# Forget heads' values computed as feature tiles inside the attention, and a new place for the bias strips' source

## The chip, the cores and the metric

The kernel runs on 1 core of one Trainium2 chip. The metric is the device time in microseconds (us) of one execution. Three executions of the kernel before took 2245.96, 2246.1 and 2246.89 us (median 2246.1).

## The reference, cut to what matters

Two blocks run one after the other on 512 tokens of width 1024. The first has two layers (L0 and L1) of attention and feed-forward, and the change touches only these and the scratch memory of the second block (M).

```python
proj = h @ w_in[l]                                   # h: 512 x 1024, normed
qa, ka, va, qb, kb, vb, f_logit = jnp.split(proj, split_at, axis=-1)   # six parts of 512, one of 8
oa = diff_attention(rotary(qa), rotary(ka), va, lam) # 4 heads, two maps each, values 128 wide
oa = rms_norm(oa, diff_sub_g[l]) * (1.0 - lam_init)
ob = forgetting_attention(qb, kb, vb, log_sigmoid(f_logit + forget_bias[l]))  # 8 heads of 64
x = x + rms_norm(concat(oa, ob) @ w_out[l], attn_post_g[l])
x = x + rms_norm((silu(h2 @ w_gate[l]) * (h2 @ w_up[l])) @ w_down[l], ffn_post_g[l])
```

The forgetting attention adds a decay to the scores, the difference of cumulated log forget gates. The second block has an attention with a relative position bias. It reads this bias from strips in device memory (8 heads x 128 rows x 512 words), which the kernel writes near its start.

## The kernel before, in words

All engines run hand-ordered programs, and waits on counters tie them together. SyncE (SP) streams 512 KB weight slabs in the order of a list, `plan`, into four raw buffers. A slab's transfer may be issued once the slab four places before it has been split. ScalarE (ACT) copies each slab to a rounded high part (L1532), and VectorE (DVE) subtracts to get the low part (L927). There are three buffers for such pairs. TensorE (PE) then makes three matmuls for each product (high by low, low by high, high by high).

Two shapes of product are used. A **token tile** (`token_tiles`, L633 to L635) holds 128 tokens by 512 columns of the output. It takes slabs of 2 x 128 rows by 512 columns, so that a row of a slab is 2 KB long. Four token tiles need 96 matmuls. A **feature tile** (`feature_tile`, L593) holds 128 columns by 512 tokens. It takes a slab of 8 x 128 rows by 128 columns, so that a row is 512 B long, and needs 24 matmuls.

In each layer PE makes the forget tile, the first tile of `qa` and of `ka` with their rotations (L735), then `va` as four token tiles, the small transposes of the log forget gates (L746), `vb` as four token tiles, and the sums of the log gates (L752). DVE copies the even token tiles into `V` (L1188), and ACT the odd ones (L1694). Both do so after they have split all slabs up to three places past the last `va` slab, or `vb` slab (`slabs_of`, `splits_for`). DVE then writes the negated sums (L1194), from which GpSimd (POOL) makes the decay rows. Slabs are counted from 0 here: forget, `qa`, `ka`, four of `va` (3 to 6), and then in the kernel before four of `vb` (7 to 10).

The attention (`attend`) runs 32 steps, steps 0 to 15 for the four differential heads and steps 16 to 31 for four pairs of forget heads, four query tiles each. In step i, PE makes the scores of step i (L661, L666), then what `fill(i)` gives it, the transposes of the weights of step i - 3 (L677), and, for every second step, the products with the values of step i - 4 (L690). Six more turns end it. `FILL` puts the remaining 14 feature tiles of `qa`, `ka`, `qb` and `kb` into the turns 0, 1, 4, 5, 8, 9, 13, 15, 17, 19, 21, 23, 25 and 27. Within a turn DVE reduces the scores to their maximum (L990 in a forget step), ACT takes the exponentials (L1583), DVE the reciprocals of the sums (L1004), POOL scales the weights (L1943), and PE transposes them. DVE and ACT copy the transposed weights to memory (L1020, L1600), and the results of the forget heads go to `MIXED` by ACT (L1609) and DVE (L1041). PSUM has eight banks: seven go round in the order of use during the attention, and the last holds the products with the values.

At its start POOL issues nine small loads for the second block (`BVR`, `BFG`, `W2C`; L1951 to L1954), and then one transfer of 2 MB that writes the bias strips (L1958). Its source is `REVB`, 8 partitions of 640 words in the arena, where rows of the attention's weights lie later. DVE and ACT therefore wait for that transfer before L0's attention.

## Time and profile before

| | |
|---|---|
| median of three executions | 2246.1 us |
| the profiled execution, its own time | 2241.13 us |
| its span, from first to last instruction | 2239.8 us |
| TensorE busy | 2119.8 us (95%) |
| VectorE, ScalarE, GpSimd busy | 988.2, 814.8, 227.0 us |
| mean granted TensorE clock | 0.987 |

The page gives the busy time of each engine and the groups of instructions; the trace behind it gives each instruction with its start and the wait before it. With TensorE busy nearly all the time, the waits on TensorE are what is to be read, and the time counts that lie between two of its landmarks. Starts are in us from the span's start.

### The profile page before, as it was taken

The page shows a single profiled execution, that of the slowest core. Times are in us where ns is not written, and L with a number is a line of the kernel's source. Part 1 is how long each engine was busy: PE and PEld are TensorE (multiplying, and loading weights), DVE is VectorE, ACT ScalarE, POOL GpSimd, SP SyncE. Part 2 cuts the span into 40 slices and gives each one's busy share as a digit, 9 for nine tenths or more (in the row PEclk, how much of TensorE's full clock was granted, in tenths as well). Part 3 has the DMA queues.
Part 4 walks back from the last instruction along what each step waited for, and adds up shares of the span by engine and source line. Part 5 has one row for each costly group of instructions (what it writes and reads, how often), then busy time and mean ns, then how long its engine had stood idle before and what let it go on. Part 6 is the DMA issues. An engine that isn't in the chain of part 4 may idle for free. (4 is left out here: it accounts for less than half of the span.)

```text
span 2239.8 us, 25576 instructions
## 1 busy us (share of the span) xinstructions
PE 2119.8 (95%) x10364; PEld 1703.8 (76%) x10364; DVE 988.2 (44%) x1833; ACT 814.8 (36%) x1574; POOL 227.0 (10%) x256
## 2 busy tenths in 40 slices
PE   6899899999998999999999998999798999999997
PEld 5667688888887767688888887878655788888886
DVE  6265453323336375453323336645456444323333
ACT  4145442222234255452222225344256334222322
POOL 3003410000000004310000000000156101000000
PEclk9999999999999999999999999999999999999999
DMA  6521123333322311223233332322411233333321
GB/s 155 110 76 57 57 73 109 97 97 97 103 86 69 108 43 63 67 84 102 92 99 97 96 98 58 98 57 81 104 43 38 67 111 92 94 97 101 94 92 68
DMA packets 273721, 192.10 MB, mean 86 GB/s; under 512 B 22060, under 2 KB 241364, under 8 KB 273604
## 3 DMA queue, kind: packets, MB, share of 16 engines
q1 hardware_dynamic: 268704, 177.76, 27.2%
q0 software_dynamic: 4752, 12.67, 2.4%
q8 instruction: 82, 1.34, 0.2%
q14 instruction: 35, 0.29, 0.0%
q10 hardware_dynamic: 148, 0.04, 0.0%
HBM read 186.21 MB, written 4.23 MB: 85 GB/s over the span
## 5 line engine op out<-in xcount | busy, mean ns | idle before, releaser
L593 PE MATMUL bank<-h_features,weights_hi_lo 128*128 128x512 f32 (+1 forms) x5160 | 1131.4, 380 | 9.5 <-POOL h_features L1915 7.8
L593 PEld LDWEIGHTS bank<-h_features,weights_hi_lo 128*128 128x128 f32 x5160 | 928.7, 189 | 196.0 <-issue 14.8
L927 DVE TENSOR_TENSOR weights_hi_lo<-weights,weights_hi_lo 128x1024 fp32r<-128x1024 f32 (+1 forms) x337 | 402.5, 1198 | 702.2 <-ACT weights_hi_lo L1532 701.7
L1532 ACT ACTIVATE weights_hi_lo<-weights 128x1024 fp32r<-128x1024 f32 (+1 forms) x337 | 341.0, 1016 | 393.1 <-PE bank L635 346.2
L633 PE MATMUL bank<-weights_hi_lo,hidden 128*128 128x512 f32 x528 | 205.4, 389 | 0.0
L634 PE MATMUL bank<-weights_hi_lo,hidden 128*128 128x512 f32 x528 | 205.4, 389 | 0.0
L635 PE MATMUL bank<-weights_hi_lo,hidden 128*128 128x512 f32 x528 | 205.4, 389 | 0.0
L1648 ACT ACTIVATE hidden<-arena 128x512 fp32r<-128x512 f32 x66 | 41.7, 632 | 300.1 <-DVE arena L1078 300.1
L1943 POOL TENSOR_SCALAR arena<-arena,row_stats 128x256 f32<-128x256 f32 (+5 forms) x140 | 126.8, 916 | 170.6 <-DVE row_stats L1004 63.4
L1915 POOL TENSOR_TENSOR h_features<-arena,h_features 128x512 fp32r<-128x512 f32 x24 | 30.7, 1278 | 988.8 <-ACT h_features L1560 988.8
L1078 DVE TENSOR_TENSOR arena<-bank,arena 128x512 f32<-128x512 f32 x66 | 45.6, 692 | 181.3 <-PE bank L593 181.3
L633 PEld LDWEIGHTS bank<-weights_hi_lo,hidden 128*128 128x128 f32 x528 | 99.1, 188 | 20.6
L635 PEld LDWEIGHTS bank<-weights_hi_lo,hidden 128*128 128x128 f32 x528 | 99.1, 188 | 20.6
L634 PEld LDWEIGHTS bank<-weights_hi_lo,hidden 128*128 128x128 f32 x528 | 99.1, 188 | 20.6
L1643 ACT ACTIVATE arena<-bank 128x512 f32<-128x512 f32 x66 | 39.5, 598 | 202.3 <-PE bank L593 202.3
L1583 ACT ACTIVATE arena<-arena,row_stats 128x256 f32<-128x256 f32 (+5 forms) x140 | 68.0, 486 | 72.7 <-DVE row_stats L990 72.4
L633 PE MATMUL bank<-weights_hi_lo,h_features 128*128 128x512 f32 (+1 forms) x192 | 74.4, 388 | 9.3 <-DVE arena L1188 5.4
L661 PE MATMUL bank<-arena 64*128 64x128 f32 (+7 forms) x384 | 71.6, 451 | 11.4 <-DVE neg_decay L1194 1.7
L990 DVE CUSTOM_DVE_ANT_0 arena<-bank,bias_rows 128x256 f32<-128x256 f32 (+5 forms) x140 | 52.0, 402 | 57.8 <-PE bank L666 29.7
L634 PE MATMUL bank<-weights_hi_lo,h_features 128*128 128x512 f32 (+1 forms) x192 | 72.8, 379 | 0.0
L635 PE MATMUL bank<-weights_hi_lo,h_features 128*128 128x512 f32 (+1 forms) x192 | 72.7, 379 | 0.0
L647 PE MATMUL bank<-diag_rstd,x_residual 128*128 128x128 f32 x384 | 48.2, 284 | 24.6 <-DVE diag_rstd L941 24.6
(335 smaller groups left out, 2053.8 us busy)
## 6 DMA issues: line engine op xcount, KB each, us to landing
weights<-in_w_in_dram SPq DMA_DIRECT2D x84, 512.0 KB, 3.9
weights<-in_w_gate_dram SPq DMA_DIRECT2D x66, 512.0 KB, 3.8
weights<-in_w_up_dram SPq DMA_DIRECT2D x66, 512.0 KB, 3.8
weights<-in_w_down_dram SPq DMA_DIRECT2D x60, 512.0 KB, 3.6
weights<-in_w_out_dram SPq DMA_DIRECT2D x24, 512.0 KB, 3.7
bias_rows<-decay_scratch POOLq DMA_DIRECT2D x16, 256.0 KB, 4.0
weights<-in_w_cmp_dram SPq DMA_DIRECT2D x16, 256.0 KB, 4.6
weights<-in_w_down_dram SPq DMA_DIRECT2D x12, 256.0 KB, 2.6
```

The costliest lines, as they stand in the source:

```text
L593: last = e.matmul(out_ap, l, r, start=(j == 0), stop=(j == len(pairs) - 1))
L633: e.matmul(outs[t][:, 0:width], sh, wl, start=(k == 0), stop=False)
L634: e.matmul(outs[t][:, 0:width], sl, wh, start=False, stop=False)
L635: last = e.matmul(outs[t][:, 0:width], sh, wh, start=False, stop=(k == kt - 1))
L647: last = e.matmul(out_ap[:, k * P:(k + 1) * P], X[:, t, (k0 + k) * P:(k0 + k + 1) * P], DIAG[:, t, :], start=True, stop=True)
L661: last = e.matmul(outs[j][:, 0:u.w], l, r, start=True, stop=u.kind == "nsa")
L927: e.tensor_tensor(pair_view(i, 1), raw_view(i), pair_view(i, 0).bitcast(F32), ALU.subtract).then_inc(done, tick(("split", i)))
L990: e.tensor_tensor_reduce(row(i, j)[:, 0:u.w], bank[:, 0:u.w], u.bias[j](BIAS[use % 4]), -1.0, u.floor, ALU.add, ALU.min, st[:, j:j + 1]).t ...
L1078: e.tensor_tensor(FULL[f % 2], bank[:, :], SILU[f % 2], ALU.mult).then_inc(done, tick((s, "product", f)))
L1532: e.activation(pair_view(i, 0), raw_view(i), ACT.Copy).then_inc(done, tick(("hi", i)))
L1583: e.activation(row(i, j)[:, 0:u.w], row(i, j)[:, 0:u.w], ACT.Exp, bias=st[:, j:j + 1], scale=-1.0, accum_out=st[:, 2 + j:3 + j]).then_inc( ...
L1943: e.tensor_scalar(row, row, st[:, 6 + j:7 + j], None, ALU.mult).then_inc(done, tick((*u.name, "scaled", j)))
```

## The change

The values of the forget heads (`vb`) are no longer made as four token tiles ahead of the attention. They become four feature tiles, in the turns 18, 22, 26 and 30 of the attention. DVE copies such a tile to one of two scratch rows, PE transposes it in four pieces a turn later, and ACT copies the result into `V`. The first product with these values waits for that copy. The transposes of the log gates move ahead of `va`, and DVE's copy of them with it. `REVB` becomes a part of `BVR`, the waits of DVE and ACT for the strips' transfer go, and POOL issues the nine small loads after L0's attention, after a wait for the strips.

```diff
@@ -89,7 +89,8 @@
 
 
 FILL = sorted([(4 * p - 4 + i, c, p) for p in range(1, 4) for i, c in enumerate((C_QA, C_KA))]
-              + [(4 * p - 3 + 2 * i, c, p - 4) for p in range(4, 8) for i, c in enumerate((C_QB, C_KB))])
+              + [(4 * p - 3 + 2 * i, c, p - 4) for p in range(4, 8) for i, c in enumerate((C_QB, C_KB))]
+              + [(4 * p + 2, C_VB, p - 4) for p in range(4, 8)])
 FILL_AT = {at: (c, m) for at, c, m in FILL}
 
 LAG = 6
@@ -252,7 +253,7 @@
         POSI = arena(8192, T).bitcast(I32)
         LAM = arena(10240, 4 * LAYERS * HD).rearrange("p (a l d) -> p a l d", a=4, l=LAYERS)
         ROWS, PER = arena(0, P), arena(128, P)
-        REVB = ARENA[0:NH, 13440:13440 + REV]
+        REVB = BVR[0:NH, 0:REV]
         BFG = NLAM[:, 8:12]
         QA, KA, QB, KB = (arena(2048 * i, 4, T) for i in range(4))
         V = arena(8192, NT, D)
@@ -347,7 +348,6 @@
             plan_features((s, "qk"), w, C_QA, P)
             plan_features((s, "qk"), w, C_KA, P)
             plan_tokens((s, "va"), w, [(C_VA, C_VA + 512)], ND)
-            plan_tokens((s, "vb"), w, [(C_VB, C_VB + 512)], ND)
             for _, c, m in FILL:
                 plan_features((s, "qk"), w, c + m * P, P)
             for half in range(2):
@@ -686,6 +686,8 @@
                         for j in range(len(u.turned)):
                             lane = dve if turned_by_vector(u, j) else act
                             pe.wait_ge(lane.done, lane[*u.name, "pt", j])
+                        if u.kind == "fox":
+                            pe.wait_ge(act.done, act[u.name[0], "values", u.p - N_DIFF])
                     for r, c0, c1, l, moving, start, stop in g.products:
                         last = e.matmul(out_ap[r, c0:c1], l, moving, start=start, stop=stop)
                     last.then_inc(done, tick(g.name))
@@ -739,13 +741,12 @@
                     feature_tile((s, "qk", C_KA), HT)
                     rotate(C_QA, 0)
                     rotate(C_KA, 0)
-                    token_tiles((s, "va"), 512, HT, ND)
                     out_ap = bank((s, "logs"))
                     pe.wait_ge(dve.done, dve[s, "log f"])
                     for t in range(NT):
                         last = e.transpose(out_ap[:, N_FOX * t:N_FOX * (t + 1)], NEGC[:, t * P:(t + 1) * P], CST[0:N_FOX, 0:N_FOX])
                     last.then_inc(done, tick((s, "logs")))
-                    token_tiles((s, "vb"), 512, HT, ND)
+                    token_tiles((s, "va"), 512, HT, ND)
                     out_ap = bank((s, "sums"))
                     pe.wait_ge(dve.done, dve[s, "logs"])
                     for t in range(NT):
@@ -756,6 +757,13 @@
                     def fill(at):
                         if at - 1 in FILL_AT and FILL_AT[at - 1][0] in (C_QA, C_KA):
                             rotate(*FILL_AT[at - 1])
+                        if at - 1 in FILL_AT and FILL_AT[at - 1][0] == C_VB:
+                            m = FILL_AT[at - 1][1]
+                            out_ap = bank((s, "values turned", m))
+                            pe.wait_ge(dve.done, dve[s, "value features", m])
+                            for t in range(NT):
+                                last = e.transpose(out_ap[:, t * P:(t + 1) * P], ROPE[m % 2][:, t * P:(t + 1) * P], IDENT)
+                            last.then_inc(done, tick((s, "values turned", m)))
                         if at in FILL_AT:
                             c, m = FILL_AT[at]
                             feature_tile((s, "qk", c + m * P), HT)
@@ -1182,20 +1190,15 @@
                     straight(C_KA, 0)
                     crossed(C_QA, 0)
                     crossed(C_KA, 0)
-                    for part, base in (("va", 0), ("vb", 512)):
-                        slabs_of((s, part), ND, 512, 1)
-                        for t in range(0, NT, 2):
-                            e.tensor_copy(V[:, t, base:base + 512], full((s, part, t))[:, :]).then_inc(done, tick())
-                            banks.leave(dve, (s, part, t))
-                        if part == "va":
-                            e.tensor_copy(FGT, full((s, "logs"))[:, 0:NT * N_FOX]).then_inc(done, tick((s, "logs")))
-                            banks.leave(dve, (s, "logs"))
-                    dve.also((s, "values"))
+                    e.tensor_copy(FGT, full((s, "logs"))[:, 0:NT * N_FOX]).then_inc(done, tick((s, "logs")))
+                    banks.leave(dve, (s, "logs"))
+                    slabs_of((s, "va"), ND, 512, 1)
+                    for t in range(0, NT, 2):
+                        e.tensor_copy(V[:, t, 0:512], full((s, "va", t))[:, :]).then_inc(done, tick((s, "values")))
+                        banks.leave(dve, (s, "va", t))
                     e.tensor_scalar(NEGC[:, :], full((s, "sums"))[0:N_FOX, :], -1.0, None, ALU.mult).then_inc(done, tick((s, "decay")))
                     banks.leave(dve, (s, "sums"))
                     dve.wait_ge(act.done, act[s, "values"])
-                    if layer == 0:
-                        dve.wait_ge(strips_written, 16)
 
                     def fill(at):
                         if at - 1 in FILL_AT and FILL_AT[at - 1][0] in (C_QA, C_KA):
@@ -1205,6 +1208,11 @@
                             splits_for((s, "qk", c + m * P))
                             if c in (C_QA, C_KA):
                                 straight(c, m)
+                            if c == C_VB:
+                                if m >= 2:
+                                    dve.wait_ge(pe.done, pe[s, "values turned", m - 2])
+                                e.tensor_copy(ROPE[m % 2], full((s, "qk", c + m * P))[:, :]).then_inc(done, tick((s, "value features", m)))
+                                banks.leave(dve, (s, "qk", c + m * P))
                         if at - 2 in HEAD_AT:
                             h = HEAD_AT[at - 2]
                             dve.wait_ge(act.done, act[s, "head rstd", h])
@@ -1688,21 +1696,23 @@
                     rope(C_QA, 0)
                     splits_for((s, "qk", C_KA))
                     rope(C_KA, 0)
-                    for part, base in (("va", 0), ("vb", 512)):
-                        slabs_of((s, part), ND, 512, 1)
-                        for t in range(1, NT, 2):
-                            e.activation(V[:, t, base:base + 512], full((s, part, t))[:, :], ACT.Copy).then_inc(done, tick((s, "values")))
-                            banks.leave(act, (s, part, t))
-                    if layer == 0:
-                        act.wait_ge(strips_written, 16)
+                    slabs_of((s, "va"), ND, 512, 1)
+                    for t in range(1, NT, 2):
+                        e.activation(V[:, t, 0:512], full((s, "va", t))[:, :], ACT.Copy).then_inc(done, tick((s, "values")))
+                        banks.leave(act, (s, "va", t))
 
                     def fill(at):
+                        if at - 1 in FILL_AT and FILL_AT[at - 1][0] == C_VB:
+                            m = FILL_AT[at - 1][1]
+                            e.activation(V[:, :, 512 + m * P:512 + (m + 1) * P], full((s, "values turned", m))[:, :].rearrange("p (t c) -> p t c", t=NT),
+                                         ACT.Copy).then_inc(done, tick((s, "values", m)))
+                            banks.leave(act, (s, "values turned", m))
                         if at in FILL_AT:
                             c, m = FILL_AT[at]
                             splits_for((s, "qk", c + m * P))
                             if c in (C_QA, C_KA):
                                 rope(c, m)
-                            else:
+                            elif c in (C_QB, C_KB):
                                 e.activation((QB if c == C_QB else KB)[:, m, :], full((s, "qk", c + m * P))[:, :], ACT.Copy,
                                              scale=SCALE if c == C_QB else 1.0).then_inc(done, tick((s, "qk", c, m)))
                                 banks.leave(act, (s, "qk", c + m * P))
@@ -1946,12 +1956,6 @@
                                     bias_rows(use, bias_of(use))
 
                 turned_norm("L0 attn")
-                for at, src in ((0, b_in[C_MV:C_MO]), (512, b_in[C_NKV + 384:C_NKV + 512]), (640, b_in[C_NKV + 640:C_NKV + 768]),
-                                (768, b_in[C_IF:C_NQ]), (776, b_in[C_NG:C_MERGE])):
-                    e.dma_start(BVR[:, at:at + src.shape[0]], src.partition_broadcast(P)).then_inc(late_in, 16)
-                e.dma_start(BFG, a["b_fgate_2"][0].partition_broadcast(P)).then_inc(late_in, 16)
-                for at, j in ((0, 0), (1, 0), (2, 1)):
-                    e.dma_start(W2C[:, at, :], a["w_cmp2_2"][0, j]).then_inc(late_in, 16)
                 rows_of = REVB[:, P - 1:P - 1 + T]
                 shifted = bass.AP(rows_of.tensor, rows_of.offset, [list(rows_of.ap[0]), [-1, P], [1, T]])
                 pool.wait_ge(dve.done, dve["strips"])
@@ -1971,6 +1975,14 @@
                             e.tensor_tensor(SQUARES, DIFF_OUT[h], DIFF_OUT[h], ALU.mult).then_inc(done, tick((s, "head squares", h)))
 
                     attend(s, ATTN_E, lambda use: decay_dram[layer, use - N_FOX * layer].partition_broadcast(P), fill)
+                    if layer == 0:
+                        pool.wait_ge(strips_written, 16)
+                        for at, src in ((0, b_in[C_MV:C_MO]), (512, b_in[C_NKV + 384:C_NKV + 512]), (640, b_in[C_NKV + 640:C_NKV + 768]),
+                                        (768, b_in[C_IF:C_NQ]), (776, b_in[C_NG:C_MERGE])):
+                            e.dma_start(BVR[:, at:at + src.shape[0]], src.partition_broadcast(P)).then_inc(late_in, 16)
+                        e.dma_start(BFG, a["b_fgate_2"][0].partition_broadcast(P)).then_inc(late_in, 16)
+                        for at, j in ((0, 0), (1, 0), (2, 1)):
+                            e.dma_start(W2C[:, at, :], a["w_cmp2_2"][0, j]).then_inc(late_in, 16)
                     gain_row(a["attn_post_g"][layer], (s, "heads"))
                     turned_norm(f"{s} ffn")
                     gain_row(a["ffn_post_g"][layer], (s, "gain row free"))
```

## Rows read from the trace of the kernel before

**Rows 1.** The page's first part: busy us, share of the span, instructions.
```profile
PE 2119.8 (95%) x10364; PEld 1703.8 (76%) x10364; DVE 988.2 (44%) x1833; ACT 814.8 (36%) x1574; POOL 227.0 (10%) x256
```
**Rows 2.** Timeline of PE, L0: start, duration, engine, line, operation, count, wait before it.
```profile
71.92 0.41 PE L746 MATMUL bank<-shape_consts,neg_decay 8*128 8x8 f32 x4
76.23 0.79 PE L633 MATMUL bank<-weights_hi_lo,h_features 128*128 128x512 f32 x1 [3.91 <-DVE weights_hi_lo L927]
...
88.45 0.79 PE L633 MATMUL bank<-weights_hi_lo,h_features 128*128 128x512 f32 x1 [5.43 <-DVE arena L1188]
...
107.87 2.32 PE L752 MATMUL bank<-shape_consts,arena 128*8 128x512 f32 x8
111.05 0.49 PE L661 MATMUL bank<-arena 64*128 64x128 f32 x4 [0.86 <-DVE neg_decay L1194]
```
**Rows 3.** Timeline of ACT, L0: the splits of slabs 7 and 8.
```profile
73.87 1.06 ACT L1532 ACTIVATE weights_hi_lo<-weights 128x1024 fp32r<-128x1024 f32 x1 [17.04 <-DMA weights<-in_w_in_dram]
85.48 1.06 ACT L1532 ACTIVATE weights_hi_lo<-weights 128x1024 fp32r<-128x1024 f32 x1 [10.56 <-DMA weights<-in_w_in_dram]
```
**Rows 4.** Timeline of DVE, L0: the copies of two `va` tiles.
```profile
87.71 1.28 DVE L1188 COPY arena<-bank 128x512 f32<-128x512 f32 x2
```
**Rows 5.** Timeline of PE, L1: the same places as in L0.
```profile
744.09 0.41 PE L746 MATMUL bank<-shape_consts,neg_decay 8*128 8x8 f32 x4
...
769.62 0.49 PE L661 MATMUL bank<-arena 64*128 64x128 f32 x4 [0.86 <-DVE neg_decay L1194]
```
**Rows 6.** Timeline of PE, L0, turn 27: four transposes, and a feature tile.
```profile
242.10 0.60 PE L677 MATMUL bank<-shape_consts,junk 128*128 128x128 f32 x4
242.63 1.13 PE L661 MATMUL bank<-arena 64*128 64x512 f32 x4
...
243.78 5.71 PE L593 MATMUL bank<-h_features,weights_hi_lo 128*128 128x512 f32 x24
249.33 0.38 PE L677 MATMUL bank<-shape_consts,arena 128*128 128x128 f32 x2
```
**Rows 7.** Timeline of PE, L0, turn 23: a transpose behind the tile.
```profile
229.84 0.33 PE L677 MATMUL bank<-shape_consts,arena 128*128 128x128 f32 x1 [1.16 <-ACT gain_row L1714]
```
**Rows 8.** Timeline of PE, L0: the attention's last turns, from the scores of step 30.
```profile
254.70 0.92 PE L661 MATMUL bank<-arena 64*128 64x384 f32 x4
...
259.95 1.73 PE L690 MATMUL bank<-token_scratch,arena 128*64 128x256 f32 x16 [1.74 <-DVE heads_features L1041]
...
271.28 0.50 PE L633 MATMUL bank<-weights_hi_lo,heads_features 128*128 128x512 f32 x1
```
**Rows 9.** Timeline of POOL, L0: scaling of steps 30 and 31, then the gain row.
```profile
261.29 4.84 POOL L1943 TENSOR_SCALAR arena<-arena,row_stats 128x384 f32<-128x384 f32 x3 [2.44 <-DVE row_stats L1004]
...
272.59 0.58 POOL L1921 DMA_DIRECT2D gain_row<-in_attn_post_g_dram  x1 [4.93 <-DVE heads_features L1041]
```
**Rows 10.** Timeline of POOL: the first small loads' issue, and the strips' issue.
```profile
35.79 2.71 POOL L1951 DMA_DIRECT2D value_bias_rows<-in_b_in_dram  x5
...
40.59 1.12 POOL L1958 DMA_DIRECT2D bias_scratch<-arena  x1
```
**Rows 11.** Timeline of DVE: the last write of the strips' source.
```profile
38.97 0.17 DVE L1156 MEMSET arena<- 8x128 f32 x1
```
**Rows 12.** DMA issues, 0 to 125 us: size of each, median us from issue to landing.
```profile
bias_scratch<-arena POOLq DMA_DIRECT2D x1, 2048.0 KB, 45.6
```
**Rows 13.** DMA queues, 67 to 74 us: packets, MB, share of 16 engines.
```profile
q0 software_dynamic: 84, 0.34, 44.8%
q1 hardware_dynamic: 84, 0.16, 5.8%
```
**Rows 14.** The page's last part: all slabs of the first block's input weights.
```profile
weights<-in_w_in_dram SPq DMA_DIRECT2D x84, 512.0 KB, 3.9
```
**Rows 15.** Windows: stretch, length, busy time of each engine, granted clock (PEclk), DMA share, GB/s.
```profile
78.00:80.00 2.00, 2.00 (x6) 1.52 (x6) 0.00 (x0) 0.00 (x0) 0.00 (x0) 0.50 0.89 188
20.30:24.00 3.70, 3.67 (x20) 3.67 (x21) 2.12 (x10) 2.35 (x3) 0.00 (x0) 1.00 0.00 0
```

## The prediction

> **What bounds the kernel now.** I read the busy shares first: TensorE is busy for 95% of the span and no other engine for half of it [rows 1]. So only what makes TensorE wait or work more can move the time. I then laid the timelines of the two layers side by side, from the small transposes (L746) to the attention's first scores (L661). In L1 this takes 769.62 - 744.09 = 25.53 us [rows 5], in L0 111.05 - 71.92 = 39.13 us [rows 2]. The work is the same, so L0 loses 13.6 us here: 3.91 and 5.43 us of waiting, and 4.3 us in matmuls at a granted 0.50, the 1.2 GHz level, after each wait [rows 2, 15].
>
> ACT's rows name the cause: slabs 7 and 8 reach it only at 73.87 and 85.48, after waits for their transfers [rows 3]. At that time the strips' transfer is in flight, issued at 40.59 [rows 10] and landed 45.6 us later, at 86.2 [rows 12]; a slab usually lands after 3.9 us [rows 14]. The copies of the `va` tiles stand behind slab 8's split, on DVE [rows 4] as on ACT, and these hold both PE's banks and the values. The reader should see here that the stall in L0 comes from the strips' traffic, and not from the wait for the strips: DVE and ACT come to that wait behind all of `vb`, some 20 us after the strips have landed. Dropping it is worth nothing by itself.
>
> **The change, part by part.** I sum against the profiled execution (2241.13 us, span 2239.8) and add the sum to the median of 2246.1, which lies 5.0 above it.
>
> *Taken away ahead of the attention.* In L1 the 25.53 us from L746 to the scores hold the transposes (0.35), `vb`, and the sums with a wait for their bank, 111.05 - 107.87 = 3.2 us as in L0 [rows 2, 5]. `vb` is the rest, 22.0. The transposes only move ahead of `va`. The sums and the wait stay: counted through the ring of banks, the attention of L1 again begins on the bank of the sums. So L1 saves 22.0 us, 22.9 if that wait goes too.
>
> *L0 is different, since the stall does not go.* Slabs 7 and 8 become the feature slabs of turns 0 and 1, still ahead of the copies of `va` on DVE and ACT. PE has finished `va` (71.92, plus 0.35 for the transposes ahead of it) and the sums (2.3) near 74.6, and then waits for the values. These come 3.6 us after slab 8 has landed: the split on ACT at 85.48, the split on DVE, two copies done at 89.0 [rows 3, 4]. The half of `vb` that PE made inside this wait before is no longer there to fill it. When does slab 8 land?
> - POOL issues the strips at about 39.2 instead of 40.59, as the nine small loads no longer stand before them (from 35.79) and DVE's last write of the source ends at 39.1 [rows 10, 11]. So the strips land near 84.8.
> - Between 67 and 74 us the strips' queue and the slabs' queue moved 84 packets each [rows 13], one for one, the strips on close to 8 of the 16 engines (44.8%). A slab of `vb` has 256 rows of 2 KB, the slab now in its place 1024 rows of 512 B, 64 for each engine. If the turns go by rows, slab 7 is not through before the strips are, and slab 8 follows. A slab alone lands in 3.9 us, latency included [rows 14]; for the rest of slab 7 and for slab 8, already queued, I put 2.5 us. This gives 87.3.
> - The low bound is the old landing less 1.4, so 84.1; the high bound is two whole slabs after the strips, 84.8 + 2 x 3.9 = 92.6. I take 87.3, as the nearest row shows turns by packet, and slab 7 has most of the strips' time to advance.
>
> The attention of L0 so starts at 87.3 + 3.6 = 90.9, not 111.05: 20.15 us earlier (87.7 and 96.2 by the bounds). PE has then been idle for 16 us. The two waits of before cost 4.3 us in clock, 2.1 each. After the idle start of the kernel it had the full clock at once [rows 15]. So the clock costs between 0 and 4.3 us; I take 2.1, as the two waits lie nearer. The Trainium skill, "TensorE: Matmul & The Clock Gate", Part 1, has the low clock as the state after any long idle. By it the cost would not be 0; the row at 20.30 speaks against it.
>
> *Added inside the attention, in each layer.* A feature tile costs 249.33 - 243.78 = 5.55 us [rows 6], less some 0.05 for the start of what follows; four are 22.0. Four transposes take 242.63 - 242.10 = 0.53 us [rows 6], or 0.5 where more follow; four times this is 2.0. Together 24.0 us. DVE's four copies and ACT's four take the place of as many taken away, and these engines are half idle. DVE's copy (0.64 us, as in [rows 4]) comes when the tile is done, while PE has transposes and the next scores before it turns the values. Behind that copy stands DVE's copy of transposed weights, which a product needs a turn later. If this cover failed, each tile would cost 0.64 us, 5.1 for the eight.
>
> *New waits for banks.* In turn 23 PE waits 1.16 us for the bank of the heads' squares, because its seventh successor in the ring comes before ACT has read it [rows 7]; in turn 19 the ring stands one place short of that. With a tile in turn 18 and the turned values in 19, the count of seven is met in turn 19 too. This adds 1.16, and 0.1 in turn 23, where the wait moves one transpose forward: 1.3 in each layer, bounds 0 and 1.4.
>
> *Gained at the end of the attention.* From the scores of step 30 to the first output matmul lie 271.28 - 254.70 = 16.6 us, the longest wait in it 1.74 us for DVE, which is behind with the bank of the products [rows 8]. The tile in turn 30 gives DVE, ACT and POOL 5.5 us to catch up. It does not help step 31, whose scores come after it: from these on, the maxima, the reciprocals of step 30 and POOL's four pieces, three of them 4.84 us [rows 9], follow one another. Worked through engine by engine this makes the stretch behind the tile 3.3 us shorter in each layer. Bounds: 1.7 (only the longest wait goes) and 5.7 (all waits and the slow clock beside them).
>
> *Moved.* The nine small loads now stand behind L0's attention on POOL, before the gain row. Their issue took 40.59 - 35.79 = 4.8 us [rows 10]. POOL is free after its last scaling and waits 4.93 us for DVE in any case [rows 9], and the gain row is first read when the first output tile is done. The second block reads these loads long after. POOL's wait for the strips is met by then. The price if this cover were gone is those 4.8 us.
>
> **The sum.** L1: -22.0 + 24.0 + 1.3 - 3.3 = 0.0. L0: -20.15 + 2.1 + 24.0 + 1.3 - 3.3 = +3.95. Together +3.95 us, so 2250.0.
>
> **Rivals.** *The slabs are not held back by their shorter rows.* If the engines that carry both change after many rows and not after each, 512 B rows cost nothing and slab 8 lands at 84.1. The attention starts at 87.7, 3.2 us sooner: +0.75, or 2246.9. For it speaks that slab 7 landed at 73.87 although it had 10 of its 16 rows per engine in the 7 us before [rows 3, 13], so it got few earlier and the turns may be lumpy; against it that in these 7 us both moved packet for packet. The Trainium skill has this rule, in "DMA: Bandwidth & Descriptors", "Queues, rings and completion order": an engine drains a packet of several descriptors from one ring before it turns to the next. By that page the time would be this rival's.
>
> *Faster.* The tile in turn 30 covers all of the attention's end (5.7 us a layer in place of 3.3), and the ring costs nothing (0 for 1.3). That is 7.4 us over the two layers: -3.45 with my landing of slab 8, and -6.65 with the early one, so 2239.5. With the early landing it decides from 4.6 us a layer on (gain at the end less ring), where I have 2.0. Against it stands the order of POOL's pieces for steps 30 and 31.
>
> *Slower.* The slabs stand behind the strips wholly, and slab 8 lands at 92.6. The attention starts at 96.2: +9.25, or 2255.4. It counts as slower from a landing at 87.9 on. For it speaks the little that slab 7 got at first; against it that it did move before the strips' end.
>
> *The change doesn't do what it says.* The moved source frees nobody: the removed wait had long been met, and in the changed kernel it would be met at 84.8, before the values are there. This is in my forecast, where the second half of the change is worth only the 1.4 us of the earlier issue.
>
> **How the numbers follow.** A change within 0.2% (4.5 us) is about what a measurement of this kernel cannot tell from none. Chances: my forecast 0.42, early slabs 0.20, faster 0.13, late slabs 0.25. The forecast's own spread (clock, end of the attention, ring) is some 2.5 us either way, so over a third of it lies above 4.5, and a small part of the early case lies below -4.5. This makes faster 0.14, same 0.46, slower 0.40. The range goes from 2240.5, which leaves part of the fast case out, to 2257.0, the late case with 1.6 us less gained at one layer's end.
>
> **What would show each step.** PE's wait before the first scores of L0 should be near 16 us and end with DVE's or ACT's copy of values; ACT's wait for slab 8 should end near 87, and the clock after it be 0.50 for some us. From L746's old place to the first scores L1 should lose 22 us. A wait of about 1.2 us should stand in turn 19 of both layers, and the stretch behind turn 30's tile should be some 3 us shorter than from the scores of step 30 before. I am wrong if slab 8 lands at its old time or earlier, if turn 30's tile is followed by no wait at all, or if DVE's new copies show up as waits of PE.

## The result: 2253.4 us, 7.5 us slower, and the profile after

| | before | after |
|---|---|---|
| median, eight executions each | 2245.9 us (2243.7 to 2246.9) | 2253.4 us (2249.0 to 2255.7) |
| ratio of the medians | | 1.0034, interval 1.0023 to 1.0045 (5.2 to 10.1 us) |
| profiled execution, own time | 2241.13 us | 2253.34 us |
| its span | 2239.8 us | 2252.0 us |
| mean granted TensorE clock | 0.987 | 0.984 |

The two profiled executions lie 12.2 us apart and the medians 7.5: that of before was 4.8 us faster than its median, that of after stands at its median. So a difference between the two traces counts only where its place and its cause can be named.

The page's first part of after, to be held against [rows 1] (busy us, share of the span, instructions):

```profile
PE 2124.5 (94%) x10396; PEld 1708.8 (76%) x10396; DVE 991.5 (44%) x1837; ACT 816.7 (36%) x1578; POOL 225.5 (10%) x256
```

TensorE still sets the time. It has 32 instructions more, the transposes of the values, and waits more. Where it waits stands in the timeline of PE in L0 of after (start, duration, engine, line, operation, count, wait before it), which answers to [rows 2] and, from 256 us on, to [rows 8]:

```profile
73.12 2.32 PE L753 MATMUL bank<-shape_consts,arena 128*8 128x512 f32 x8
90.94 0.80 PE L661 MATMUL bank<-arena 64*128 64x128 f32 x4 [15.50 <-DVE arena L1197]
91.83 7.89 PE L593 MATMUL bank<-h_features,weights_hi_lo 128*128 128x512 f32 x24
...
197.88 0.33 PE L677 MATMUL bank<-shape_consts,arena 128*128 128x128 f32 x1 [1.16 <-ACT gain_row L1724]
...
225.44 0.44 PE L677 MATMUL bank<-shape_consts,arena 128*128 128x128 f32 x2 [1.26 <-ACT gain_row L1724]
...
256.32 0.92 PE L661 MATMUL bank<-arena 64*128 64x384 f32 x4
...
257.27 5.71 PE L593 MATMUL bank<-h_features,weights_hi_lo 128*128 128x512 f32 x24
262.82 0.60 PE L677 MATMUL bank<-shape_consts,arena 128*128 128x128 f32 x4
...
269.24 0.52 PE L677 MATMUL bank<-shape_consts,arena 128*128 128x128 f32 x3 [0.70 <-POOL arena L1953]
271.55 0.87 PE L692 MATMUL bank<-arena 128*64 128x256 f32 x8 [1.80 <-DVE heads_features L1049]
...
275.08 1.73 PE L692 MATMUL bank<-token_scratch,arena 128*64 128x256 f32 x16 [1.64 <-DVE heads_features L1049]
276.75 0.50 PE L633 MATMUL bank<-weights_hi_lo,heads_features 128*128 128x512 f32 x1
```

PE has done all that stands before the attention at 75.4 (73.12 + 2.32) and then waits 15.5 us for the values. The wait's cause is in the timeline of ACT of after, the splits of slabs 7 and 8, which answer to [rows 3]:

```profile
85.89 1.06 ACT L1540 ACTIVATE weights_hi_lo<-weights 128x1024 fp32r<-128x1024 f32 x1 [27.86 <-DMA weights<-in_w_in_dram]
87.37 1.06 ACT L1540 ACTIVATE weights_hi_lo<-weights 128x1024 fp32r<-128x1024 f32 x1 [0.43 <-DMA weights<-in_w_in_dram]
```

Slab 7 comes 12 us later than before, slab 8 only 1.9 us later. The DMA queues of after between 67 and 74 us, which answer to [rows 13], show why (packets, MB, share of 16 engines):

```profile
q0 software_dynamic: 86, 0.35, 48.4%
q1 hardware_dynamic: 85, 0.04, 2.0%
```

Both queues again move one packet each in turn. A packet of the slabs is one row, which is now 512 B and not 2 KB, so the slabs get 0.04 MB where they had 0.16. A packet of the strips holds 4 KB in both kernels (0.34 MB in 84 packets, 0.35 in 86).

In the table below, a layer is cut at three landmarks, all starts in PE's timelines: the first `va` matmul, the attention's first scores, and the first output matmul. Before, the small transposes stand behind `va`, and so inside the first stretch; after, they stand ahead of it, and 0.35 us is added for them.

| from the first `va` matmul to the output, us | scores begin after | attention | sum | against before |
|---|---|---|---|---|
| L0 before | 61.42 | 160.23 | 221.65 | |
| L0 after | 39.81 + 0.35 | 185.81 | 225.97 | +4.3 |
| L1 before | 47.81 | 161.77 | 209.58 | |
| L1 after | 25.17 + 0.35 | 184.70 | 210.22 | +0.6 |

The landmarks of L1 in after, in its timeline of PE (the first `va` matmul, then the first scores):

```profile
728.08 0.50 PE L633 MATMUL bank<-weights_hi_lo,h_features 128*128 128x512 f32 x1
...
753.25 0.49 PE L661 MATMUL bank<-arena 64*128 64x128 f32 x4 [0.86 <-DVE neg_decay L1199]
```

So 5.0 us are lost between these landmarks, nearly all in L0. The medians differ by 7.5.

### The profile page after: what moved, and what is told of

Same layout as the page of the kernel before. It is cut to its first block and busy times, and to the rows that moved or that the text cites. A ratio compares the mean times of both kernels' runs of the same rounds, so it can differ in the third digit from the quotient of the medians.

```text
span 2252.0 us, 25637 instructions
## 1 busy us (share of the span) xinstructions
PE 2124.5 (94%) x10396; PEld 1708.8 (76%) x10396; DVE 991.5 (44%) x1837; ACT 816.7 (36%) x1578; POOL 225.5 (10%) x256
## 5 line engine op out<-in xcount | busy, mean ns | idle before, releaser
L593 PE MATMUL bank<-h_features,weights_hi_lo 128*128 128x512 f32 (+1 forms) x5352 | 1180.1, 381 | 9.4 <-POOL h_features L1925 7.7
L593 PEld LDWEIGHTS bank<-h_features,weights_hi_lo 128*128 128x128 f32 x5352 | 966.3, 189 | 203.9 <-issue 14.7
L1953 POOL TENSOR_SCALAR arena<-arena,row_stats 128x256 f32<-128x256 f32 (+5 forms) x140 | 125.1, 904 | 220.6 <-DVE row_stats L1012 109.1
L661 PE MATMUL bank<-arena 64*128 64x128 f32 (+7 forms) x384 | 73.0, 459 | 26.0 <-DVE arena L1197 15.5
L647 PE MATMUL bank<-diag_rstd,x_residual 128*128 128x128 f32 x384 | 48.9, 286 | 24.4 <-DVE diag_rstd L949 24.4
L677 PE MATMUL bank<-shape_consts,arena 128*128 128x128 f32 (+2 forms) x364 | 62.9, 285 | 9.4 <-ACT gain_row L1724 6.8
L647 PEld LDWEIGHTS bank<-diag_rstd,x_residual 128*128 128x128 f32 x384 | 46.4, 199 | 27.6 <-DVE diag_rstd L949 27.3
L677 PEld LDWEIGHTS bank<-shape_consts,arena 128*128 128x128 f32 (+2 forms) x364 | 42.0, 140 | 32.9 <-issue 12.1
```

The lines of the kernel that those rows point to most:

```text
L593: last = e.matmul(out_ap, l, r, start=(j == 0), stop=(j == len(pairs) - 1))
L647: last = e.matmul(out_ap[:, k * P:(k + 1) * P], X[:, t, (k0 + k) * P:(k0 + k + 1) * P], DIAG[:, t, :], start=True, stop=True)
L661: last = e.matmul(outs[j][:, 0:u.w], l, r, start=True, stop=u.kind == "nsa")
L677: last = e.transpose(out_ap[0:n, c:c + P], rows[j][:, c:c + n], IDENT)
L1953: e.tensor_scalar(row, row, st[:, 6 + j:7 + j], None, ALU.mult).then_inc(done, tick((*u.name, "scaled", j)))
```

## The experiments

Each edit is given against the kernel before or after, as named. Ratios are to the kernel before, run on the same chip.

**Which half of the change does it.** The kernel after with the strips' half undone:

```diff
-        REVB = BVR[0:NH, 0:REV]
+        REVB = ARENA[0:NH, 13440:13440 + REV]
...
+                    if layer == 0:
+                        dve.wait_ge(strips_written, 16)
```

(ACT waits likewise, and the nine small loads stand again ahead of the strips.)

> The changed kernel with its second half undone: the strips' source is back in the arena, the nine small loads stand ahead of the strips' issue, and DVE and ACT wait for the strips before L0's attention. My theory (the cost is the strips' traffic on the slabs with 512 B rows, and the tiles inside the attention): the second half is worth only its earlier issue, so this is 0 to 1.5 us slower than the changed kernel, some 8 us over the kernel before, and PE's wait before L0's first scores is 16 to 17 us. Rival (the moved loads on POOL are what costs): this kernel is at or near the time of the kernel before.

Measured: 2252.55 us, ratio 1.0040 (1.0027 to 1.0052). PE's wait in its timeline, L0 of this kernel:

```profile
92.01 0.80 PE L661 MATMUL bank<-arena 64*128 64x128 f32 x4 [17.02 <-DVE arena L1197]
```

And the kernel before with the strips' half alone:

```diff
-        REVB = ARENA[0:NH, 13440:13440 + REV]
+        REVB = BVR[0:NH, 0:REV]
...
-                    if layer == 0:
-                        dve.wait_ge(strips_written, 16)
```

> The kernel before with the second half of the change alone: source in the other buffer, no waits of DVE and ACT, small loads behind L0's attention. My theory: slabs 7 and 8 land about 1 us earlier, 0 to 1.5 us faster than the kernel before, and no new wait at the end of L0's attention. Rival (the moved loads cost 4.8 us of POOL in the open, or collide with output slabs): 3 to 5 us slower.

Measured: 2244.26 us, ratio 1.0002 (0.9993 to 1.0011). PE's two waits of [rows 2] stand as before, in its timeline of this kernel:

```profile
77.18 0.78 PE L633 MATMUL bank<-weights_hi_lo,h_features 128*128 128x512 f32 x1 [3.63 <-DVE weights_hi_lo L927]
...
89.01 0.79 PE L633 MATMUL bank<-weights_hi_lo,h_features 128*128 128x512 f32 x1 [5.88 <-DVE arena L1188]
```

The tiles make the whole loss that can be told. The strips' half alone gains nothing that shows (0 to 1.5 us were expected). Behind the tiles it may be worth a microsecond (1.0040 against 1.0034), which is inside the intervals and so not shown.

**Whether the strips' transfer is the cause of the stall.** Both kernels again, with the strips written in 32 pieces of four rows a head, one in each turn of L0's attention, and so all behind the slabs. The kernel before needs the strips' half for it, since its source lies in the arena:

```diff
-                shifted = bass.AP(rows_of.tensor, rows_of.offset, [list(rows_of.ap[0]), [-1, P], [1, T]])
-                e.dma_start(strip_dram, shifted).then_inc(strips_written, 16)
+                def strip_piece(at):
+                    r0 = STRIP_ROWS * (at - STRIP_FIRST)
...
+                    if at >= 1:
+                        pool.wait_ge(dve.done, dve[*STEPS["L0"][0][at - 1].name, "norm"])
+                    e.dma_start(strip_dram[:, r0:r0 + STRIP_ROWS, :], shifted).then_inc(strips_written, 16)
```

> The changed kernel with the strips' transfer cut into 32 pieces of 4 rows for each head, one issued in each turn of L0's attention, so that none of it runs while slabs 7 and 8 are fetched. My theory: PE's wait of 15.5 us before L0's first scores and the 2.6 us at half clock behind it go, 18 us less than the changed kernel, 10 us under the kernel before. Rival (the traffic's cost is only moved, each piece delays a slab inside the attention): the gain is given back there in waits of PE for splits, and the time stays within 5 us of the changed kernel.

> The kernel before with the second half of the change and the same 32 pieces. My theory: L0's stretch from L746 to the first scores takes 25.5 us as in L1, instead of 39.1, so 13.6 us less than the kernel before, 2232. The difference to the changed kernel with paced strips is then the cost of the tiles inside the attention alone, about 2 us in each layer, 3 to 5 us in all. Rival (the tiles cost nothing, the whole loss came from the strips): both paced kernels have the same time.

Measured: after with pieces 2233.53 us, ratio 0.9954 (0.9941 to 0.9966); before with pieces 2229.9 us, ratio 0.9935 (0.9923 to 0.9948). PE's timeline of after with pieces, L0, has no wait at all ahead of the scores:

```profile
73.37 2.32 PE L753 MATMUL bank<-shape_consts,arena 128*8 128x512 f32 x8
75.62 0.49 PE L661 MATMUL bank<-arena 64*128 64x128 f32 x4
```

and that of before with pieces has L1's 25.5 us from the small transposes to the scores:

```profile
72.48 0.41 PE L746 MATMUL bank<-shape_consts,neg_decay 8*128 8x8 f32 x4
...
97.99 0.46 PE L661 MATMUL bank<-arena 64*128 64x128 f32 x3 [0.86 <-DVE neg_decay L1194]
```

The strips' traffic beside the slabs is the cause. Spreading it out gives the kernel before 14 us and the kernel after 18 (1.0034 less 0.9954). This is net of what the pieces cost inside L0's attention: from the first scores to the output, before with pieces takes 162.0 us (97.99 to 260.03) where before takes 160.2. Without the stall the change still is no gain: after is then 3.6 us behind before, and all five times of after lie above all five of before (2232.7 to 2236.8 against 2226.1 to 2231.9).

**Whether the length of a slab's row matters by itself.** The kernel before, whose `vb` slabs now come as four transfers of 128 columns, with rows of 512 B, and are used as before:

```diff
-            plan_tokens((s, "vb"), w, [(C_VB, C_VB + 512)], ND)
+            plan_tokens((s, "vb"), w, [(C_VB + P * c, C_VB + P * (c + 1)) for c in range(4)], ND)
```

> The kernel before, in which each slab of the forget heads' values is fetched by four transfers of 128 columns, so in rows of 512 B instead of 2 KB, into the same buffer. The work is unchanged. My theory (engines that carry strips and slabs take turns by row): slab 7 lands at 87 instead of 73.9 and slab 8 near 89, when the strips are through; PE waits some 16 us in one piece instead of 3.9 and 5.4, and the stretch of L0 from L746 to the first scores is 4 to 7 us longer. Rival (turns of many rows, or by bytes): slabs 7 and 8 land as before, at 74 and 85.5, and the time is that of the kernel before.

Measured: 2247.58 us, ratio 1.0012 (1.0003 to 1.0021). ACT's timeline of this kernel, slabs 7 and 8:

```profile
86.47 1.06 ACT L1532 ACTIVATE weights_hi_lo<-weights 128x1024 fp32r<-128x1024 f32 x1 [29.51 <-DMA weights<-in_w_in_dram]
88.17 1.06 ACT L1532 ACTIVATE weights_hi_lo<-weights 128x1024 fp32r<-128x1024 f32 x1 [0.64 <-DMA weights<-in_w_in_dram]
```

and PE's timeline has one wait for slab 7 in place of two:

```profile
88.84 0.79 PE L633 MATMUL bank<-weights_hi_lo,h_features 128*128 128x512 f32 x1 [16.37 <-DVE weights_hi_lo L927]
```

Slab 7 goes from 73.87 to 86.47, within 0.6 us of its place in the kernel after. The bytes, the buffers and the engines' work are those of before. The edit changes two things at once, the row length and the number of transfers for a slab (four for one). In the kernel after, a slab with such rows comes as a single transfer and is as late, so the row length is what they have in common. From the small transposes to the first scores L0 now takes 43.5 us (72.06 to 115.54), 4.4 more than before, as expected (4 to 7).

The DMA queues of this kernel, 74 to 78 us (packets, MB, share of 16 engines), show one for one again:

```profile
q0 software_dynamic: 48, 0.20, 46.6%
q1 hardware_dynamic: 48, 0.02, 2.0%
```

From 67 to 74 us, however, they moved 84 and 253 packets. Two new transfers of a slab's part were issued in these 7 us. The equal counts hold while an old transfer is being finished; a new one begins with a burst, probably on the engines that carry no strips, but the counts do not name the engines.

**What the order of the copies is worth.** The kernel after, with the copies of `va` ahead of the splits of slabs 7 and 8 on DVE and on ACT:

```diff
-                    slabs_of((s, "va"), ND, 512, 1)
+                    splits(SLAB_AT[s, "va", 6] + 1)
                     for t in range(0, NT, 2):
                         e.tensor_copy(V[:, t, 0:512], full((s, "va", t))[:, :]).then_inc(done, tick((s, "values")))
                         banks.leave(dve, (s, "va", t))
+                    splits_for((s, "va", 6))
```

> The changed kernel with the copies of the va tiles ahead of the splits of slabs 7 and 8 on DVE and ACT. My theory: the values are ready at 75, the first scores of L0 are no longer held, but the tile of turn 0 then waits for slab 7 itself, which lands near 86 and is split at 88; PE's wait moves from the scores to the tile and is 2 to 4 us shorter. So the landing of the slabs, not the order of the copies, is most of the stall. Rival (the order of the copies makes the stall): the 15.5 us go nearly all.

Measured: 2250.17 us, ratio 1.0031 (1.0021 to 1.0042). PE's timeline of this kernel, L0 and then L1:

```profile
75.77 0.49 PE L661 MATMUL bank<-arena 64*128 64x128 f32 x4
...
88.61 8.11 PE L593 MATMUL bank<-h_features,weights_hi_lo 128*128 128x512 f32 x24 [12.13 <-DVE weights_hi_lo L935]
...
755.04 0.49 PE L661 MATMUL bank<-arena 64*128 64x128 f32 x4 [2.46 <-DVE neg_decay L1200]
```

The scores now start at 75.8, and the wait moves behind them: turn 0's tile needs slab 7, whatever the order. In L1 the reordered copies hold up the decay and cost 1.6 us. What stalls is the slab, and no queue of instructions.

**The waits for banks.** The kernel after with the value tiles in the turns 16, 20, 24 and 30:

```diff
-              + [(4 * p + 2, C_VB, p - 4) for p in range(4, 8)])
+              + [(at, C_VB, m) for m, at in enumerate((16, 20, 24, 30))])
```

> The changed kernel with the value tiles in the turns 16, 20, 24 and 30 instead of 18, 22, 26 and 30, so that the bank of the heads' squares is again seven places from one that is free. My theory: the wait of 1.16 us in turn 19 goes in both layers and that of turn 23 stays near 1.2, 2.4 us less than the changed kernel in all. Rival (the wait in turn 19 comes from ACT's load beside the tile in turn 18, not from the ring): a wait of the same size appears in turn 17 or 21 and the time does not change.

Measured: 2249.34 us, ratio 1.0019 (1.0008 to 1.0029). 2.4 us less than the kernel after was expected; the two ratios (1.0034 and 1.0019) differ by 3.4, with some 3.5 to either side. Turn 19's wait is gone, turn 23's is that of before, in the timeline of PE, L0, and so in L1:

```profile
223.78 0.33 PE L677 MATMUL bank<-shape_consts,arena 128*128 128x128 f32 x1 [1.16 <-ACT gain_row L1724]
```

**The end of the attention.** Two edits of the kernel after. The first puts the split of the first output slabs five turns later:

```diff
-LAST_STEP, LAST_STEP_2 = 32, 48
+LAST_STEP, LAST_STEP_2 = 37, 48
```

> The changed kernel with one number edited: the split of the third output slab stands in turn 37, behind the attention's last products, and not in turn 32. My theory for the waits that were left at the attention's end (1.80 and 1.64 us for DVE): DVE and ACT spend some 3 us on this split while the transposed weights and the bank of the products wait behind it. Then the waits for DVE shrink and each layer gains about 2 us, 4 in all. Rival (POOL's scaling of steps 30 and 31 ends this stretch, as I wrote in the prediction): PE then waits for POOL instead and the gain is under 1 us in all.

Measured: 2247.65 us, ratio 1.0012 (1.0003 to 1.0021). The rest of the waits behind turn 30's tile, in the timeline of PE of this kernel, L0:

```profile
269.52 0.52 PE L677 MATMUL bank<-shape_consts,arena 128*128 128x128 f32 x3 [0.70 <-DVE token_scratch L1028]
...
272.51 0.66 PE L677 MATMUL bank<-shape_consts,junk 128*128 128x128 f32 x4 [0.89 <-POOL junk L1953]
273.95 1.73 PE L692 MATMUL bank<-token_scratch,arena 128*64 128x256 f32 x16 [0.78 <-ACT token_scratch L1608]
275.61 0.50 PE L633 MATMUL bank<-weights_hi_lo,heads_features 128*128 128x512 f32 x1
```

From the scores of step 30 (256.61) to the output this is 19.0 us in both layers, where the kernel after has 20.43 in L0 and 21.94 in L1. That is 4.4 us in all, and the ratios differ by 4.9 (1.0034 and 1.0012); some 4 were expected. PE's waits for DVE's products (1.80 and 1.64) are gone, and POOL comes next.

The second takes the tile out of the end, by putting it into turn 28:

```diff
-              + [(4 * p + 2, C_VB, p - 4) for p in range(4, 8)])
+              + [(at, C_VB, m) for m, at in enumerate((18, 22, 26, 28))])
```

> The changed kernel with its last value tile in turn 28 instead of 30. In the trace of the changed kernel the end of the attention, from the scores of step 30 to the first output matmul less the tile and its transposes, is 2.1 us shorter than before in L0. My theory: this gain belongs to the tile's place. With the tile in turn 28 the stretch behind the scores of step 30 is 16 to 17 us again, as before, and the kernel is 2 to 4 us slower than the changed one. Rival (the end of the attention does not depend on the tile's place): the same time as the changed kernel.

Measured: 2253.13 us, ratio 1.0039 (1.0027 to 1.0052). By the ratios this is 1 us slower than the kernel after, where 2 to 4 were expected, but the interval of that difference is some 4 us to either side. The timeline of PE, L1, from the scores of step 30:

```profile
926.29 0.92 PE L661 MATMUL bank<-arena 64*128 64x384 f32 x4
...
931.54 1.74 PE L692 MATMUL bank<-token_scratch,arena 128*64 128x256 f32 x16 [1.73 <-DVE heads_features L1049]
...
942.87 0.50 PE L633 MATMUL bank<-weights_hi_lo,heads_features 128*128 128x512 f32 x1
```

16.58 us, to the hundredth what the kernel before has in L0 [rows 8], with the same waits. L0 of this kernel takes 18.10, as L1 of before takes 18.09, more of each at the lower clock (granted 0.83 and 0.81). That the tile in turn 30 gains something at the end is read from this trace. It is not shown by the median.

**Both kernels without strips' traffic, early splits and bank waits.** Before with pieces and `LAST_STEP, LAST_STEP_2 = 37, 53`; after with pieces, the same, and the turns 16, 20, 24 and 30.

> The kernel before with the moved source, the strips in 32 pieces, and the early splits at the ends of the three attentions put behind their last products. My theory: the paced kernel's 2229.9, less 1 to 2 us for each of the two layers and about 1 for the second block's attention: 2226 to 2228. Rival (these splits were hidden, or are missed by the output tiles when they come late): 2230 or more, with a wait of PE for a split at the output tiles.

> The changed kernel with the same pieces and late splits, and with its tiles in the turns 16, 20, 24 and 30. The gains found one by one are 2.4 us (turns) and 4 to 5 us (late splits) on the paced kernel's 2233.5, so 2226 to 2228 if they add up. My theory: the tiles inside the attention then cost no more than they cover, and the two paced kernels lie within 1.5 us of each other. Rival (a token tile ahead of the attention stays the cheaper place, by transposes and by nothing to cover): the kernel before with the same edits is faster by 3 us or more.

Measured: 2224.64 us, ratio 0.9913 (0.9900 to 0.9927), and 2223.61 us, ratio 0.9915 (0.9901 to 0.9928). These are the fastest kernels of the study, some 20 us under the kernel before, and both under the 2226 to 2228 that was expected. They are equal within some 4 us to either side. With the other costs away, moving `vb` into the attention neither gains nor loses anything that shows.

## Why the prediction was right in most of its working, and its likeliest case did not come

The time, 2253.4, lies in the range; the likeliest case, within 0.2%, did not come, and slower by over 0.2%, which had 0.40, did. Step by step:

- **The landing of slab 8 and the start of L0's attention: right.** 87.3 was forecast and 87.37 read, the attention at 90.9 and 90.94, the idle time 16 and 15.5. This execution issued the strips at 40.10 us, having run 0.7 us late from its first matmuls on; with that taken off, the slab came 0.6 sooner than the sum has it. The turns by row, on which this rested, are shown twice: by the 86 and 85 packets, and by the 512 B rows in the kernel before. That the strips hold the slabs at all is shown by the stall's end once they are out of the way. The rival of the early slabs (84.1) is refuted, and that of the late ones (92.6) too. The Trainium skill, "DMA: Bandwidth & Descriptors", "Queues, rings and completion order", lets an engine turn to another ring after each packet, and gives some 9 to 17 descriptors as a packet's usual size. The trace agrees with the first (86 and 85 packets), but not with that size: here a packet of the slabs is a single row (0.04 MB in 85). By the size that the Trainium skill's page gives, the 64 rows that an engine has of a slab would have passed in 4 to 7 turns, an estimate from its figures. In the traces the row length moved slab 7 by 12.6 us.
- **The clock after the stall: 2.1 forecast, some 2.7 measured.** The first 18.1 us after the stall, 91.0 to 109.1, were granted 0.85 on average, all the loss of it in the first 6:

```profile
91.00:97.00 6.00, 6.00 (x19) 4.74 (x20) 2.18 (x4) 1.75 (x5) 2.60 (x5) 0.54 0.52 139
97.20:101.00 3.80, 3.80 (x19) 2.44 (x18) 0.61 (x2) 0.60 (x1) 0.00 (x0) 1.00 0.96 280
```

  (Windows of after, with columns as in [rows 15].) One long stall pays nearly what each of the two short ones paid. That two became one is what the forecast said. The lower bound of 0, however, rested on a wrong reading. The row at 20.30 [rows 15] shows 1.00 in the column of the clock, but also only 20 matmuls in 3.67 us, 0.18 us each. The next window of before has the same transposes (L647) at 0.11 each:

```profile
24.00:29.20 5.20, 5.17 (x47) 4.98 (x45) 4.25 (x6) 3.78 (x5) 2.54 (x2) 1.00 0.00 0
```

  So TensorE did not have its full rate at once after the idle start, and the row does not speak against a cost of the clock after a long idle time. The column reads 1.00 there in all 13 traces, whatever the rate, and cannot be used for these first microseconds.
- **L1's stretch ahead of the attention: -22.0 forecast, -22.3 measured** (25.17 + 0.35 against 47.81).
- **Tiles and transposes: 24.0 a layer forecast, 23.7 measured.** The tile of turn 30 takes 262.82 - 257.27 = 5.55 us, the four transposes of turned values 0.36 to 0.44 and not 0.5. DVE's and ACT's new copies hold up nobody, as forecast.
- **The bank waits: right.** 1.16 more in turn 19 and 0.1 more in turn 23, in both layers; with the tiles in other turns both additions are gone.
- **The end of the attention: the term that was mis-sized.** 3.3 us a layer were forecast and 2.1 came. From the scores of step 30 to the output L0 has 276.75 - 256.32 = 20.43 us, and before 16.58; with a tile and its transposes of 5.95 us in it, the end gained 5.95 - 3.85 = 2.1. L1 gives the same (both kernels take 1.5 us more there, at a lower granted clock: 18.09 and 21.94). The 2.1 are also of another kind than forecast. The tile was to shorten waits, and PE's waits in this stretch of L0 went only from 4.59 to 4.14 us. The rest is the clock, 0.90 before and 1.00 after. The windows from the scores of step 30 to the output, before and then after:

```profile
254.70:271.28 16.58, 11.99 (x83) 7.26 (x81) 8.38 (x22) 8.26 (x22) 10.44 (x9) 0.90 0.09 33
```

```profile
256.32:276.75 20.43, 16.30 (x111) 11.25 (x109) 10.51 (x24) 9.82 (x24) 14.19 (x18) 1.00 0.24 71
```

  What the working overlooked is in the timeline of DVE of after:

```profile
267.50 0.17 DVE L1012 RECIPROCAL row_stats<-row_stats 128x2 f32<-128x2 f32 x1 [0.78 <-ACT junk L1591]
269.30 1.53 DVE L935 TENSOR_TENSOR weights_hi_lo<-weights,weights_hi_lo 128x1024 fp32r<-128x1024 f32 x1 [1.63 <-ACT weights_hi_lo L1540]
270.75 0.41 DVE L1028 COPY arena<-bank 128x256 f32<-128x256 f32 x1
271.09 0.41 DVE L1049 TENSOR_TENSOR heads_features<-bank,heads_features 128x256 fp32r<-128x256 f32 x1
```

  The split of an output slab belongs to turn 32, and so stands behind turn 30's tile. DVE waits 1.63 us for ACT's half of it and works 1.53 us on it, and the copies that PE waits for come after. I had let the tile cover this. With the split five turns later the stretch is 19.0 us, 3.5 less than before has with the early split, near the 3.3 of the sum. The kernel before loses by that split too. Before with pieces and late splits has this window in L1:

```profile
900.11:915.40 15.29, 10.68 (x82) 6.48 (x80) 7.23 (x21) 7.31 (x21) 9.63 (x9) 1.00 0.01 1
```

  That is 15.29 us at granted 1.00, for 18.09 at 0.81 in L1 of before (16.58 at 0.90 in L0). PE's waits are as long as they were (4.50 for 4.60 us), so here nearly the whole gain of 2.8 us stands in the clock. In all six such stretches with a late split the granted clock is 1.00; of the twenty with an early one it is below 1.00 in seventeen (0.73 to 0.92). How the split's place brings this about was not tried. So it is a loss of both kernels, which the tile failed to hide.
- **The moved loads: nothing that shows, as forecast.** They are issued at 272.2, behind POOL's last scaling. The strips' earlier issue was forecast at 1.4 us and was 0.5 in the traces (40.10 for 40.59, or 1.2 with the late start taken off); the two ratios, 1.0040 and 1.0034, allow it and do not show it.

The sum of the layers was +3.95 us (L0 3.95, L1 0.0), and measured it is +5.0 (4.3 and 0.6); the ends are 2.4 us worse than forecast and the clock 0.6, the transposes 0.6 better and the stretches ahead of the attention 1.4, most of it in L0, whose `va` began 1.1 us late in this trace beside slabs that were not late by as much. The layers alone would so give 2251.0, just beyond the bound of 4.5 us. The rest, 2.5 us, lies where the change alters no instruction. In the second block one wait is longer, as the waits of PE in the whole run show (before first, then after; us in total, times, longest):

```profile
PE bank L881 <- ACT arena L1851: 2.3, 2, 1.9
```

```profile
PE bank L889 <- ACT arena L1861: 3.0, 2, 2.7
```

In all eight traces with value tiles its longest is 2.7 to 3.2 us, and in all five without them 1.8 to 2.0. It is about 1 us that the forecast did not have. The ring of banks stands at another place when the second block begins, which could be the reason, but this was not tried. The last 1.5 us are inside the interval (5.2 to 10.1) and have no cause that I can name. In the two profiled executions the second block's attention, whose code is the same, took 144.3 us at granted 0.95 and 147.6 at 0.93, from its first scores to its last products; over all traces it took 143.2 to 147.6.

The forecast was 3.4 us off, and its 3.95 us lay close under the bound of 4.5. The two things that it left out, the split at turn 32 and the longer wait in the second block, were both losses. With the stretch ahead of L0's attention shorter than forecast by 1.1 us, partly because PE came to it late in this trace, the nearness of the sum of the two layers (3.95 and 5.0) is in part luck.

## What to carry to other kernels

Before work is moved ahead of or behind a slow transfer, count the packets of what shares its engines, not the bytes: a 2 MB transfer from eight partitions held a slab of 512 B rows for the rest of its 45 us, and writing it in 32 pieces inside a long loop took 14 us off the kernel before. A stall of a bounding engine isn't shortened by taking away the work that stands in it; the kernel gains there only what ends the wait. At the end of a software pipeline look for steps tied to a turn's number (splits, loads) and ask what stands behind them on the engine: moving one by five turns gave 4.4 us between the landmarks of the two layers, and 4.9 by the ratios.

## What the hardware showed that I had not expected

- **The turns hold at both ratios of sizes that were tried.** Packets of 4 KB of the strips alternate one for one with 2 KB rows of the slabs (84 and 84 in 7 us) and with 512 B rows (86 and 85). ACT waited 27.9 us for slab 7, and a slab usually lands in 3.9 [rows 14].
- **The clock's cost did not grow in proportion to the idle time.** Waits of 3.9 and 5.4 us cost 2.1 us each [rows 2], and one of 15.5 us cost 2.7.
- **Equal code runs at other rates from one execution to the next.** The first transposes of the kernel (L647, 64 of them) took 8.85 us in the trace of before, and 9.16 to 10.15 in the twelve others, with the same instructions there. Such phases make single traces differ by some microseconds (the second block's attention by 4), and terms of one or two could be told only between landmarks.
